# First tile's queries ahead of the second's, six query slabs loaded outside the ring, and a new order of the vector work behind them

## The reference, cut to what matters

```
q = x @ wq                                  # [256, 2048] @ [2048, 8 heads * 256]
s = q . subkeys                             # per head two lists of 128 key scores
s1, i1 = top_k(s[.., 0, :], 16);  s2, i2 = top_k(s[.., 1, :], 16)
top_s, pos = top_k(s1 + s2 over all 256 pairs, 16);  idx = i1 * 128 + i2 at pos
gate = softmax(top_s)                       # 8 * 16 = 128 experts for each token
act = gelu(x . u_tab[idx]);  out = sum over the 128 of (gate * act) * v_tab[idx]
```

## Time and profile before

| | |
|---|---|
| median of 3 runs | 3488.22 us (3486.0 to 3488.73) |
| the profiled execution | 3485.73 us, its span 3483.8 us |
| TensorE busy | 2611.6 us, 75% of the span |
| VectorE busy | 2464.6 us, 71% |
| GpSimd busy | 1068.8 us, 31% |
| ScalarE busy | 825.2 us, 24% |
| DMA | 1024.40 MB, mean 294 GB/s |

### The profile page before, as it was taken

How to read it: one execution, slowest core, us unless ns; L and a number is a source line. 1 busy time by engine, 2 the same in 40 slices (tenths; PEclk the granted TensorE clock), 3 DMA queues, 4 the chain that set the end, 5 groups by cost and what they waited for, 6 DMA issues and landing times. The chain is left out here.

```text
span 3483.8 us, 26996 instructions
## 1 busy us (share of the span) xinstructions
PE 2611.6 (75%) x10346; PEld 1777.7 (51%) x10346; DVE 2464.6 (71%) x2522; ACT 825.2 (24%) x790; POOL 1068.8 (31%) x652
## 2 busy tenths in 40 slices
PE   8999999323324610015567999999999999999999
PEld 4444574111111200002224888788788788888887
DVE  4865646888899899987776887678756544444565
ACT  2001231100000010000002333355433433333332
POOL 5540002877676588876652000000000000000000
PEclk9999999666667855557768999999999999999999
DMA  6887447999999999999997998455556555555775
GB/s 208 315 318 254 154 164 291 417 421 410 422 407 421 419 409 422 422 422 422 422 422 298 320 321 298 151 164 165 197 203 249 170 192 188 186 192 190 262 264 189
DMA packets 329954, 1024.40 MB, mean 294 GB/s; under 512 B 33528, under 2 KB 34040, under 8 KB 263036
## 3 DMA queue, kind: packets, MB, share of 16 engines
q1 hardware_dynamic: 255948, 486.01, 40.7%
q0 software_dynamic: 73904, 537.04, 37.2%
HBM read 1016.12 MB, written 6.86 MB: 294 GB/s over the span
## 5 line engine op out<-in xcount | busy, mean ns | idle before, releaser
L391 DVE TENSOR_TENSOR slab_low<-ring,slab_high 128x2048 fp32r<-128x2048 f32 x220 | 504.2, 2292 | 488.5 <-ACT slab_high L384 488.4
L384 ACT CAST slab_high<-ring 128x2048 fp32r<-128x2048 f32 x284 | 542.2, 1910 | 891.2 <-PE bank L370 722.1
L1876 POOL DMA_INDIRECT pool<-in_peer_u,pool x236 | 471.3, 1997 | 333.6 <-DVE pool L1613 224.3
L368 PE MATMUL bank<-slab_high,left_high 128*128 128x512 f32 x1408 | 551.4, 392 | 10.0 <-DVE res L1701 4.7
L370 PE MATMUL bank<-slab_high,left_low 128*128 128x512 f32 x1408 | 549.1, 390 | 0.0
L369 PE MATMUL bank<-slab_low,left_high 128*128 128x512 f32 x1408 | 548.9, 390 | 0.0
L1663 DVE CUSTOM_DVE_ANT_0 pool<-pool,nat 128x2048 f32<-128x2048 f32 x232 | 524.9, 2290 | 31.3 <-DMA pool<-in_peer_u,pool 30.4
L2368 PE MATMUL bank<-pool,causal 128*128 128x512 f32 x304 | 192.7, 793 | 467.3 <-ACT causal L2067 287.7
L1674 DVE SCALAR_TENSOR_TENSOR res<-pool,res 128x2048 f32<-128x2048 f32 x179 | 420.9, 2351 | 132.2 <-DMA pool<-in_peer_v,pool 118.2
L1876 POOL DMA_INDIRECT pool<-in_peer_v,pool x256 | 421.4, 1646 | 231.5 <-PE bank L2368 130.0
L2368 PEld LDWEIGHTS bank<-pool,causal 128*128 128x128 f32 x304 | 74.6, 256 | 585.1 <-issue 488.8
(11 more groups left out here) (605 smaller groups left out, 3118.5 us busy)
## 6 DMA issues: line engine op xcount, KB each, us to landing
ring<-in_w_in SPq DMA_DIRECT2D x148, 1024.0 KB, 5.1
ring<-in_w_ffn_in SPq DMA_DIRECT2D x88, 1024.0 KB, 5.0
ring<-in_w_ffn_out SPq DMA_DIRECT2D x44, 1024.0 KB, 5.1
ring<-in_w_out SPq DMA_DIRECT2D x32, 1024.0 KB, 5.1
nat<-in_w_ada SPq DMA_DIRECT2D x64, 512.0 KB, 5.5
ring<-in_w_ada SPq DMA_DIRECT2D x24, 1024.0 KB, 7.0
pool<-in_w_ada SPq DMA_DIRECT2D x24, 1024.0 KB, 8.4
ring<-in_peer_wq SPq DMA_DIRECT2D x16, 1024.0 KB, 5.2
```

What stands on the lines that cost most here:

```text
L368: nc.tensor.matmul(o, lh, high[:, part, k, :], start=first, stop=False)
L384: nc.scalar.copy(high[:, n % PARTS], ring[:, g % SLOTS]).then_inc(high_done, 1)
L391: eng.tensor_tensor(dst, ring[:, g % SLOTS], high[:, n % PARTS].bitcast(F32), ALU.subtract)\
L1876: g.indirect_dma_start(dst, None, a[table][0], bass.IndirectOffsetOnAxis(idx[:, t, n:n + 1], 0))\
```

## The change

1. Query slabs 4, 5, 6, 7, 12 and 13 get slots of their own in `left_scratch` instead of ring slots. They share the semaphores of the front's two extra slots. SP waits once for the end of the `w_out` product ahead of slab 4, for slab 4 or 5 to land ahead of slabs 6 and 7, and for slab 6 or 7 to land ahead of 12 and 13.
2. In block 0 PE multiplies tile 0 on all four slabs first. Tile 0's transposes and scores then come between the second tile's products of slab 0, and tile 1's stay where both were. ACT follows in the same order. Scores are counted one more (`QB + 1`).
3. DVE's order is new from `keys_of_block(0, 0)` on: routing pieces stand between half groups of 4 rows, `keys_of_block(0, 1)` comes behind 8 dot rows, `mix_rows_ready` goes from before `keys_of_block(0, 2)` to before `keys_of_block(0, 3)`, tile 1's first keys and pairs come earlier, and DVE waits for query slab 13 to be used ahead of `pairs_of_block(0, 2)`. The rest of tile 0's sums and the final steps are interleaved likewise (the part of the diff left out: the same calls, moved by a few groups of rows).

```diff
+        QUERY_EXTRA = {4: WIDE, 5: WIDE + 1, 6: WIDE + 2, 7: WIDE + 3, 12: WIDE, 13: WIDE + 1}
+        query_slots = [view(aTs[:, i * SLAB:(i + 1) * SLAB], [KS, NB]) for i in (2, 3, 0, 1)]
+        landed += [landed[SLOTS], landed[SLOTS + 1]] * 2
...
+            m = g - first_slab[PEER_Q]
+            if m in QUERY_EXTRA:
+                return QUERY_EXTRA[m]
...
+            if slot_of(g) >= WIDE:
+                return query_slots[slot_of(g) - WIDE]
...
-                transfers[slot_of(g)] += 16 * count
-                reach.append(transfers[slot_of(g)])
+                at = slot_of(g) if slot_of(g) < WIDE else SLOTS + slot_of(g) % 2
+                transfers[at] += 16 * count
+                reach.append(transfers[at])
...
+                sp.wait_ge(slabs_used, gq)
                 for m in range(SLOTS, KS * QB):
+                    if m in (6, 7):
+                        sp.wait_ge(landed[slot_of(gq + m)], reach[gq + m - 2])
+                    if m in (12, 13):
+                        sp.wait_ge(landed[slot_of(gq + m)], reach[gq + m - 6])
                     issue(sp, PEER_Q, m, gq + m)
...
                 keys_of_block(0, 0)
                 pairs_of_block(0, 0)
                 experts_of_block(0, 0)
-                first_dots(0, 4)
+                first_dots(0, GB)
                 keys_of_block(0, 1)
-                first_dots(4, 6)
+                dots_of(0, 1, 2)
                 pairs_of_block(0, 1)
-                first_dots(6, GB)
+                dots_of(0, 2, 2.5)
+                gate_differences(0, block_heads(0))
                 experts_of_block(0, 1)
-                gate_differences(0, block_heads(0))
-                dots_of(0, 1, 3)
+                dots_of(0, 2.5, 4)
                 softmax(0, 0, block_heads(0))
-                dots_of(0, 3, 5)
+                dots_of(0, 4, 5)
+                block_weights(0)
                 gate_differences(0, block_heads(1))
-                dots_of(0, 5, 6)
-                block_weights(0)
+                dots_of(0, 5, 6.5)
                 softmax(0, 1, block_heads(1))
-                dots_of(0, 6, 8)
-                sums_of(0, 0, 1)
-                mix_rows_ready()
+                dots_of(0, 6.5, 8)
+                sums_of(0, 0, 0.5)
                 keys_of_block(0, 2)
-                sums_of(0, 1, 2)
+                sums_of(0, 0.5, 1)
+                dve.wait_ge(slabs_used, gq + 14)
                 pairs_of_block(0, 2)
+                sums_of(0, 1, 1.5)
                 experts_of_block(0, 2)
-                sums_of(0, 2, 3)
+                sums_of(0, 1.5, 3)
                 gate_differences(0, block_heads(2))
                 block_weights(1)
                 sums_of(0, 3, 4)
                 dots_of(0, 8, 10)
                 softmax(0, 2, block_heads(2))
                 dots_of(0, 10, 12)
-                sums_of(0, 4, 5)
+                sums_of(0, 4, 4.5)
+                mix_rows_ready()
                 keys_of_block(0, 3)
-                sums_of(0, 5, 6)
+                sums_of(0, 4.5, 5)
                 pairs_of_block(0, 3)
+                sums_of(0, 5, 5.5)
                 experts_of_block(0, 3)
-                sums_of(0, 6, 7)
+                sums_of(0, 5.5, 6.5)
+                keys_of_block(1, 0)
+                sums_of(0, 6.5, 7)
+                pairs_of_block(1, 0)
+                sums_of(0, 7, 7.5)
                 gate_differences(0, block_heads(3))
                 block_weights(2)
-                sums_of(0, 7, 8)
-                keys_of_block(1, 0)
-                dots_of(0, 12, 13)
-                pairs_of_block(1, 0)
-                dots_of(0, 13, 14)
+                sums_of(0, 7.5, 8)
+                dots_of(0, 12, 14)
...
                 softmax(0, 3, block_heads(3))
-                dots_of(0, 14, 15)
+                dots_of(0, 14, 16)
+                sums_of(0, 8, 9)
+                block_weights(3)
                 experts_of_block(1, 0)
...
                 keys_of_block(1, 1)
-                block_weights(3)
-                sums_of(0, 9, 10)
+                sums_of(0, 9.5, 10)
...
-                            g.wait_ge(s_sc, QB)
+                            g.wait_ge(s_sc, QB + 1)
...
+                    act.wait_ge(s_sc, b + 2 if b else tiles[-1] + 1)
...
-                take_queries(0)
-                copy_queries(0)
-                copy_scores(0)
+                for t in range(TT):
+                    act.wait_ge(slabs_used, gq + KS) if t else act.wait_ge(s_skT, 2)
+                    nc.scalar.copy(q_blk[:, t, :], ps[t][:, :]).then_inc(s_q, 1)
+                    act.wait_ge(s_qT, t + 1)
+                    nc.scalar.copy(qT[:, :, t * P:(t + 1) * P], view(ps[4 + t][:, :], [KS, P])).then_inc(s_qTc, 1)
+                    copy_scores(0, [t])
...
+                def first_query_transposes(t):
+
+                    pe.wait_ge(s_q, t + 1)
+                    for k in range(KS):
+                        last = nc.tensor.transpose(ps[4 + t][:, k * P:(k + 1) * P], q_blk[:, t, k * P:(k + 1) * P],
+                                                   ident[:, :])
+                    last.then_inc(s_qT, 1)
...
+                    elif (j, k, t) == (KS - 1, KS - 1, 0):
+                        last.then_inc(s_skT, 1)
...
-                pe.wait_ge(s_add, TT * OB)
-                query_products(0, 0, range(KS), [1])
-                query_products(0, 1, range(KS), [1])
+                query_products(0, 2, range(KS), [0])
                 norm_transposes(2, 1)
                 norm_transposes(3, 1)
-                query_products(0, 2, range(KS))
                 pe.wait_ge(s_sk, 16)
                 for i in range(2):
                     last = nc.tensor.transpose(ps[3][:, i * P:(i + 1) * P], sk_nat[:, i, :], ident[:, :])
                 last.then_inc(s_skT, 1)
-                query_products(0, 3, range(KS))
+                query_products(0, 3, range(KS), [0])
+                pe.wait_ge(s_add, TT * OB)
+                query_products(0, 0, range(2), [1])
+                first_query_transposes(0)
+                query_products(0, 0, range(2, KS), [1])
+                block_scores(0, [0])
+                for j in range(1, KS):
+                    query_products(0, j, range(KS), [1])
                 pe.wait_ge(s_skc, 1)
                 for b in range(1, QB):
                     if b >= 2:
                         pe.wait_ge(s_q, 2 * (b - 1))
                     query_products(b, 0, range(0, 1))
-                    query_transposes(b - 1)
+                    if b == 1:
+                        first_query_transposes(1)
+                    else:
+                        query_transposes(b - 1)
                     query_products(b, 0, range(1, 2))
-                    block_scores(b - 1)
+                    if b == 1:
+                        block_scores(0, [1])
+                    else:
+                        block_scores(b - 1)
                     query_products(b, 0, range(2, KS))
```

More of the change, by code:

```diff
@@ L1659, in dots_of @@
                     q = 2 * t
-                    for m in range(lo * GB, hi * GB):
+                    for m in range(int(lo * GB), int(hi * GB)):
                         row = home(q, m)
@@ L1773, in _ @@
                 dots_of(0, 10, 12)
-                sums_of(0, 4, 5)
+                sums_of(0, 4, 4.5)
+                mix_rows_ready()
                 keys_of_block(0, 3)
-                sums_of(0, 5, 6)
+                sums_of(0, 4.5, 5)
                 pairs_of_block(0, 3)
+                sums_of(0, 5, 5.5)
                 experts_of_block(0, 3)
-                sums_of(0, 6, 7)
+                sums_of(0, 5.5, 6.5)
[3 more added lines that the diff above has]
+                sums_of(0, 7, 7.5)
                 gate_differences(0, block_heads(3))
                 block_weights(2)
-                sums_of(0, 7, 8)
-                keys_of_block(1, 0)
-                dots_of(0, 12, 13)
-                pairs_of_block(1, 0)
-                dots_of(0, 13, 14)
+                sums_of(0, 7.5, 8)
+                dots_of(0, 12, 14)
                 softmax(0, 3, block_heads(3))
-                dots_of(0, 14, 15)
+                dots_of(0, 14, 16)
+                sums_of(0, 8, 9)
+                block_weights(3)
                 experts_of_block(1, 0)
-                dots_of(0, 15, 16)
-                sums_of(0, 8, 9)
+                sums_of(0, 9, 9.5)
                 keys_of_block(1, 1)
-                block_weights(3)
-                sums_of(0, 9, 10)
+                sums_of(0, 9.5, 10)
                 pairs_of_block(1, 1)
@@ L1797, in _ @@
                 experts_of_block(1, 1)
-                sums_of(0, 11, 12)
+                sums_of(0, 11, 11.5)
                 keys_of_block(1, 2)
-                sums_of(0, 12, 13)
+                sums_of(0, 11.5, 12.5)
                 pairs_of_block(1, 2)
+                sums_of(0, 12.5, 13)
                 experts_of_block(1, 2)
```

(31 more changed lines are left out.)

## The result

The changed kernel takes 3470.03 us (median of 5 runs, 3466.94 to 3471.53) against 3487.2 us for the one before. The ratio is 0.9948 with a 95% interval of 0.9938 to 0.9959, so it is faster by 14 to 22 us. The profiled execution took 3466.94 us, the fastest of the five.

What follows compares the result with a forecast made beforehand. The DMA alone bounds one long gather stage, set by start, bytes and holes. 16.0 + 5.0 + 5.7 - 9 = 17.7 us less gives 3468.0 us profiled, forecast 3469 as median; range 3457 to 3480.

Steps and rivals of the forecast that it cites:

- Block 0's scores and the first gather: Query stage: tile 0's earlier scores start DVE's routing at 526.3 and the first gather at 542.2, gaining 16.0 us.
- Slabs moved ahead of the gathers: Query slab loads: two fewer share the full DMA stage, gaining 5.0 us; bounds nothing and 5.0.
- Holes removed: Gather stage: splitting DVE's routing lumps recovers 5.7 of 8.7 us, with 3 remaining; bounds 8.7 and a loss of 3.
- The hole at row 34: Block 1's v rows: the later mix_rows_ready delays PE's row 34, stops POOL 18 us and loses 9 us.
- bounds of 1 and 12: Row 34's loss: 1 us if seven buffers cover 17.4 us of transfers, 12 by the earlier 9.72 us stop.
- At nothing: SP's and DVE's new waits, moved gate, weight and softmax steps, and final steps: priced at no cost.
- No hole at row 34: Block 1's v rows: queued gathers cover the stop or rows take longer; gain 27 to 30 us, about 3460; chance 0.25.
- Given back by DVE's pace: Tile 0: DVE, not the DMA, sets the pace, so the earlier start is partly lost; about 3478 us; chance 0.18.
- The starved slabs: Query stage: late slabs beside gathers delay the last scores and gather 35; slower, 3502 us with scores at 680; chance 0.05.

Runs made afterwards that it cites:

- e4: The kernel before with only the query slab slots changed (slabs 4 to 7, 12 and 13 in left_scratch): 3477.78 us, ratio 0.9971.
- e5: The changed kernel with all query slabs back in the four ring slots: 3481.29 us, ratio 0.9979.
- e1: The changed kernel with mix_rows_ready moved back ahead of keys_of_block(0, 2): 3464.81 us, ratio 0.9932.
- e2: The changed kernel with PE's row products moved behind block 1's v rows and ACT's row copies behind block 2's gelu and block 1's diagonals: 3463.73 us.
- e3: The kernel before with mix_rows_ready alone moved, behind the first half group of block 1's v rows: 3497.49 us, ratio 1.0028.
- e6: The changed kernel with DVE's order of before, only the added wait for slab 13 kept: 3472.52 us, ratio 0.9958.
- e8: The changed kernel with mix_rows_ready behind dots_of(0, 8, 10) and experts_of_block(1, 0) four rows earlier: 3463.01 us, ratio 0.9928.
- e7: The kernel before with only tile 0's queries ahead, keeping the four ring slots and DVE's order: 3478.77 us, ratio 0.9970.

## Why the prediction was right

The forecast of 3469 stands 1 us from the median of 3470.03. The start, the slabs and the chain behind `mix_rows_ready` came as forecast; that the sum fits to 1 us is partly luck, since errors of up to 3 us in single terms cancel. Step by step:

*Block 0's scores and the first gather: 16.0 us expected.* 17.5 measured, 16.2 without the stages ahead. Right: DVE's start 524.86 for 526, first gather 540.74 for 542.2, last scores 626.6 to 628.6 for 631.

*Slabs moved ahead: 5.0 us.* Two slabs left the stage (SP's rows above), as said, and e4 and e5 show four slabs to be worth 9.5 us and 10 to 13. Right in size per slab. In the changed kernel alone this term can't be separated from the holes.

*Holes removed: 5.7 us.* The mechanism was right, the size too small: of the 8.7 us, 0.3 is left in the changed kernel. Part of this is owed to the new hole, which lets DVE catch up. With that one gone, e1 has 3.2 us in the two windows shown, near the 3 that I took as remaining, and 1.3 more at 1540.

*The hole at row 34: 9 us lost.* 8.7 us in the windows, a stop of 18.83 for 18. Shown three times: e1 and e2 take it out, each by another link, and e3 puts it into the kernel before. As a price on the whole kernel it is 4.8 in the stage of the changed kernel (the other holes move in) and 9.5 by the medians of e3.

The 9 itself was a choice between bounds of 1 and 12, not a result of the working, and that it fits to 0.3 us is luck. The bound of 1 took seven outstanding gathers for 17.4 us of transfers. The windows of the changed kernel around the stop show less:

```profile
891.00:903.00 12.00, 7.16 (x8) 2.48 (x8) 11.05 (x36) 2.75 (x5) 0.14 (x1) 0.50 1.01 419
903.00:904.00 1.00, 0.00 (x0) 0.00 (x0) 0.93 (x1) 0.99 (x2) 0.00 (x0) 0.50 0.47 197
904.00:911.00 7.00, 6.54 (x12) 3.01 (x13) 6.79 (x13) 1.10 (x4) 0.93 (x1) 0.74 0.03 13
```

And those of the kernel before, at its stop of 9.72 us:

```profile
951.00:963.00 12.00, 9.92 (x16) 3.83 (x15) 11.48 (x20) 0.40 (x1) 2.28 (x2) 0.72 0.99 414
963.00:964.00 1.00, 0.56 (x2) 0.00 (x0) 0.90 (x2) 0.34 (x1) 0.83 (x1) 1.00 0.27 115
```

POOL's last gather ahead of the stop ends at 891.15 in the one and at 951.12 in the other, and the DMA runs dry 12 us later in both. So the gathers under way covered about 12 us here, the length of five transfers and not of seven. The cover differs from stop to stop: the DMA begins to run short 14 us behind POOL's last gather at e6's stop of 15.87 us, 11 at e5's of 18.27 and 8 at e8's of 8.17. The stop of 18.83 leaves the DMA nearly empty for 7 us, from 904 to 911, and the way into and out of it costs the rest of the 8.7. e5's stop of 13.10 us, which cost 0.9, fits that too.

That the stop came out at 18.83 us for 18 also hides two errors that cancel. Row products and copies took 7.8 us (894.79 to 902.57) for the 5.2 taken, so that row 34 started 20.2 us behind row 32 and not 17.6. The granted clock of that stretch was 0.50, the level of 1.2 GHz, while the 5.2 came from rows at a mean of 0.79:

```profile
894.79:901.95 7.16, 7.16 (x8) 2.46 (x8) 6.99 (x34) 1.76 (x3) 0.00 (x0) 0.50 1.02 421
```

And POOL's last gather ahead of the stop ended 6.9 us behind row 32, not 4.8.

*At nothing:* e6, beside e7, shows one cover that I had not priced. `keys_of_block(0, 1)` in its old place costs 8 us once the slabs are moved, and the prediction took its new place only as a reason for the full 5.0.

The terms named so far do not close. Two slabs less (5.0), 8.4 us of holes less and 8.7 more would make the stage 4.7 us shorter, and it is 2.75. Most of the 2 us left over lie at its end: in the last 20 us ahead of SP's load the DMA moves 348 GB/s in the changed kernel (1826.4 to 1846.4) and 386 in the one before (1846.6 to 1866.6), which is 20 x 38/422 = 1.8 us. The prediction had no term for that, and no run shows its cause.

*The rivals.* No hole at row 34: false, the hole is there; e1 shows what that rival's world would have given, 3464.8 for the 3460 named. Given back by DVE's pace: false, the windows from 1150 to 1540 are whole, and e4 shows the slabs' bytes to count. The starved slabs: not in the changed kernel, where PE waits for no slab; in e5 they are late and the gathers under way hide all but about 1 us. In the Trainium skill, DMA: Bandwidth & Descriptors, section "Queues, rings and completion order", the turns packet by packet gave 12 us for a slab beside gathers, an estimate that takes the packets of the profile for those of the rule. e5's slabs come at 619.50, 631.24 and 643.09, 11.7 and 11.9 us apart, and so agree.

## What to carry to other kernels

Where one resource is full for a long stage, count the stage as its start plus its bytes plus its holes, and price every edit in these three; bytes that can move into an idle stretch ahead are worth their whole transfer time (2.49 us for each MB here). Before a step is moved later in a hand-written order, follow what stands behind its consumers in every other engine's queue: 1.3 us of vector work, moved by some 60 rows, stopped the gathers for 18.8 us through PE's and ACT's order. Parts of a change that look independent can cover for each other: early slabs alone gave 10 us and early queries alone 10, the two together 16, and 23 to 25 with a vector order that fits.

## What was not expected of the hardware

How fast the queue of gathers fills again after a stop goes with what DVE does when it ends. At 909.98 in the changed kernel DVE was among short routing instructions and the first gathers took 0.93 to 0.94 us each, 1.24 apart: twice the DMA's pace of 2.49. After the lump of before, with DVE back on full rows, the first took 2.99 us. In e1 too, a stop of 4.81 us at 904.6 ended with a gather of 3.00 us. The Trainium skill, SBUF — State Buffer, section "Who interferes with whom", says that the ports which the two engines share are an exclusive lock, and that a DVE instruction with two SBUF inputs contends with a GpSimd instruction that reads SBUF. The rows agree, with 0.94 us beside short instructions and 3.00 beside rows of 2.35; no run here separates the port from other causes. What it is worth in time is not shown either: the stops of 18.83, 18.09 and 18.27 us in the changed kernel, e3 and e5 cost 8.7, 9.1 and 11.3 us, though gathers of 0.94 us came first or second behind all three.
